# Three embedding products of the expert stage, put at other places in the instruction order

## The reference, cut to what matters

```python
h = h + hier_moe(rms_norm_2(h, g_ffn), w_rg, w_re, w1, w3, w2)
h = h + rms_norm_2(p @ w_ple, g_ple) * jax.nn.sigmoid(rms_norm_2(h, g_plg) @ w_plg)

def expert_block(args):          # for each block of tokens and its expert e
    xb, e = args
    hdn = jax.nn.silu(xb @ w1[e]) * (xb @ w3[e])
    return hdn @ w2[e]
```

## Time and profile before

| what | value |
|---|---|
| median of 3 runs | 1590.42 us (1586.77 to 1594.16) |
| the profiled execution | 1589.49 us, its span 1587.5 us |
| busy share of the span: PE, DVE, ACT, POOL | 96%, 45%, 33%, 10% |
| mean traffic, whole span | 196 GB/s |
| traffic from 1128 us to 1463 us | 420 to 421 GB/s |
| 1 MB weight loads from SP, issue to landing | 10.2 us median |

### The profile page before, as it was taken

How to read it: one execution, slowest core, us unless ns; L and a number is a source line. 1 busy time by engine, 2 the same in 40 slices (tenths; PEclk the granted TensorE clock), 3 DMA queues, 4 the chain that set the end, 5 groups by cost and what they waited for, 6 DMA issues and landing times.

```text
span 1587.5 us, 19637 instructions
## 1 busy us (share of the span) xinstructions
PE 1524.3 (96%) x7802; PEld 1065.2 (67%) x7802; DVE 717.9 (45%) x1208; ACT 530.8 (33%) x910; POOL 163.4 (10%) x172
## 2 busy tenths in 40 slices
PE   5899999999999999999999988999999999999898
PEld 5666688889888888888777766745444444444367
DVE  5344423455444444468665787532132132132174
ACT  4334422354332423345355676431011011010042
POOL 1013110002111111111300210011000000000000
PEclk9999999999999999999999999999999999999999
DMA  7111332213222222222110222779999999999951
GB/s 273 37 70 60 144 108 104 95 60 114 107 106 82 104 84 102 106 93 84 52 52 27 102 112 80 304 289 390 421 422 421 421 421 420 420 420 420 422 237 54
DMA packets 45437, 311.22 MB, mean 196 GB/s; under 512 B 5136, under 2 KB 5648, under 8 KB 10016
## 3 DMA queue, kind: packets, MB, share of 16 engines
q1 hardware_dynamic: 42336, 296.22, 46.8%
q0 software_dynamic: 3008, 13.72, 2.4%
HBM read 301.52 MB, written 8.39 MB: 195 GB/s over the span
## 4 chain that ended last, share of the span: by engine, by line
PE 88%; DVE 4%; ACT 3%; DMA 3%; issue 2%; DVEq 0%; ACTq 0%; POOLq 0%
PE bank L788 21%; PE bank L2463 14%; PE bank L832 8%; PE bank L1389 7%; PE bank L2479 6%; PE bank L841 5%; PE bank L2446 4%; PE bank L2496 4%; PE bank L2662 3%; PE bank L1246 3%; DMA M<-in_w 2%; PE bank L801 2%; PE bank L858 1%; PE bank L1782 1%; PE bank L717 1%
## 5 line engine op out<-in xcount | busy, mean ns | idle before, releaser
L612 DVE TENSOR_TENSOR w_lo<-M,w_hi 128x2048 fp32r<-128x2048 f32 x73 | 168.7, 2317 | 177.8 <-ACT w_hi L607 177.8
L2463 PE MATMUL bank<-M 128*64 128x512 f32 x1024 | 227.4, 595 | 4.3 <-DMA M<-in_w 4.3
L607 ACT ACTIVATE w_hi<-M 128x2048 fp32r<-128x2048 f32 x73 | 139.0, 1912 | 148.4 <-PE bank L788 56.9
L788 PE MATMUL bank<-HTH,w_hi 128*128 128x512 f32 x432 | 168.1, 389 | 0.0
L788 PE MATMUL bank<-HTL,w_hi 128*128 128x512 f32 x432 | 168.1, 389 | 0.0
L788 PE MATMUL bank<-HTH,w_lo 128*128 128x512 f32 x432 | 168.0, 389 | 0.0
L2463 PEld LDWEIGHTS bank<-M 128*64 128x64 f32 x1024 | 71.3, 137 | 140.0 <-issue 138.8
L2479 PE MATMUL bank<-M 128*64 128x512 f32 x512 | 114.0, 595 | 1.8 <-DMA M<-in_w 1.8
L2621 DVE TENSOR_TENSOR X<-bank,X 128x512 f32<-128x512 f32 x69 | 46.6, 689 | 113.8 <-PE bank L2496 113.7
L788 PEld LDWEIGHTS bank<-HTH,w_hi 128*128 128x128 f32 x432 | 81.1, 188 | 16.9
L788 PEld LDWEIGHTS bank<-HTL,w_hi 128*128 128x128 f32 x432 | 81.1, 188 | 16.8
(11 more groups left out here) (365 smaller groups left out, 2846.2 us busy)
## 6 DMA issues: line engine op xcount, KB each, us to landing
M<-in_w SPq DMA_DIRECT2D x192, 1024.0 KB, 10.2
M<-in_wd SPq DMA_DIRECT2D x78, 1024.0 KB, 4.8
M<-in_nb SPq DMA_DIRECT2D x4, 1536.0 KB, 6.6
X<-in_x SPq DMA_DIRECT2D x4, 512.0 KB, 9.9
M<-in_rows POOLq DMA_DIRECT2D x4, 512.0 KB, 6.2
M<-in_tb POOLq DMA_DIRECT2D x8, 256.0 KB, 4.0
rowb<-in_rows POOLq DMA_DIRECT2D x4, 512.0 KB, 5.2
xs_parts<-XSH POOLq DMA_DIRECT2D x1, 2048.0 KB, 10.1
```

Source lines behind the costliest of these rows:

```text
L607: e.activation(hi[:, :], slots[slot_of[n]], ACT.Copy).then_inc(split_hi_done, 1)
L612: e.tensor_tensor(lo[:, :], slots[slot_of[n]], hi[:, :], ALU.subtract).then_inc(split_lo_done, 1)
L788: m = e.matmul(out[:, :], w[:, k0 + k, n0:n0 + 128], v[k], start=(k == 0 and i == 0), stop=(k == len(hi) - 1 and i == 2))
L2463: m = e.matmul(b[64 * s:64 * s + 64, :], Xe[:, 4 * kh + k, o + C * s:o + C * s + C], unit_w(key, 4)[:, k, :], start=(kh == 0 and k == 0), ...
```

## The change

The three products that stood between the first gather and the steps of pairs 0 and 1 stand elsewhere: ("pl", 2, 1) behind the second quarter of group 1's gather and ahead of ("down", 0), ("pl", 3, 0) behind ("up", 1, 2) and its gather, and ("pl", 3, 1) behind ("up", 3, 2). ("pl", 2, 1) takes its PSUM bank from the common rotation instead of the routing's list. Nothing is computed differently, and each byte is moved as often as before.

```diff
-        MOE = [("one_hot", 0)] + [("gx", 0, kp) for kp in range(4)] + [("pl", 2, 1)]
+        MOE = [("one_hot", 0)] + [("gx", 0, kp) for kp in range(4)]
...
             if i == 0:
-                MOE += steps_of(0, 0) + [("pl", 3, 0)] + steps_of(0, 1) + [("pl", 3, 1), ("gs", 0), ("gs", 1), ("one_hot", 1), ("tu", 0)]
-                MOE += steps_of(1, 0) + gather(0) + steps_of(1, 1) + gather(1) + steps_of(1, 2) + gather(2, 3) + turned
+                MOE += steps_of(0, 0) + steps_of(0, 1) + [("gs", 0), ("gs", 1), ("one_hot", 1), ("tu", 0)]
+                MOE += steps_of(1, 0) + gather(0) + steps_of(1, 1) + gather(1) + [("pl", 2, 1)] + steps_of(1, 2) + gather(2, 3) + turned
...
-            MOE += steps_of(p, 0) + gather(0) + scatter(i - 2, 5) + steps_of(p, 1) + scatter(i - 2, 6, 7)
+            late = [[("pl", 3, n)] if i == 1 else [] for n in range(2)]
+            MOE += steps_of(p, 0) + gather(0) + late[0] + scatter(i - 2, 5) + steps_of(p, 1) + late[1] + scatter(i - 2, 6, 7)
...
-            if what == "gx" and at[0] == 0 or (what, *at) == ("pl", 2, 1):
+            if what == "gx" and at[0] == 0:
```

## The result

The changed kernel takes 1594.85 us in the median of 20 runs (1590.44 to 1597.71), the kernel before 1589.32 us in 20 runs (1583.73 to 1594.25). The ratio is 1.0031, with a 95% interval of [1.0022, 1.004]: within the half per cent that was called "same", in the range, and 1.9 us above the forecast of 1593 us. By the ratio the change costs 4.9 us, where 2.7 was forecast. That the median comes as near to 1593 is in part luck: the three runs that the forecast built on have a median 1.1 us above that of all 20. The profiled execution took 1591.9 us, forecast 1592.2; it is the fourth fastest of its 20, so that agreement is luck too.

A forecast was written before the change was run, and what follows sets the result against it. The weight stream was taken to set the end: load 36 0.7 us earlier, plus 3.4 us for POOL's transfers, gives +2.7 us, so 1592.2 us profiled and a median of 1593 us, 0.17% slower; range 1587 to 1598 us.

The forecast's parts named there:

- same: Outcome class: within about 0.5% (8 us) of the kernel before, what a measurement can tell from no change; chance 0.90.
- What bounds the kernel: Expert stage: the weight stream, full from 1128 us, sets the end; 1 us later there moves the end 1 us.
- PE's path: Start of expert stage: first step 1.0 us earlier after a 0.7 us wait, ("up", 1, 1) 4.8, ("up", 3, 2) 1.0 earlier.
- Load 31: Weight load waiting for the first half of ("up", 3, 2): issued at 1110.0 us, landing 4.8 us later.
- POOL's transfers: Store of tile 3 and gain load, issued near 1118 us in the full stream, cost it 3.4 us.
- The rival of hidden transfers: POOL's transfers fit between weight packets near 1118 us, load 36 lands 0.7 us earlier, median 1589.7 us; chance 0.2.
- the head start counts whole: Rival: the 4.8 us gained at ("up", 1, 1) go on into the weight stream, 1585.6 us; chance 0.08.
- The rival that the store of tile 2 holds DVE: DVE's selection for group 2 waits for a slow store, costing 1.7 us more, 1595 us; chance 0.12.
- the first step stays where it was: Rival: a wait for ACT's copy keeps the first step at 1048.5 us; median 1594 us; chance 0.1.
- 0.7 us earlier than before: Load 36, without POOL's transfers, lands at 1127.3 us instead of 1128.02 us.
- The store of tile 2 was to fit into a hole: Issued near 1086 us, before loads 23 and 24, at no cost; without the hole 1.7 us.
- nothing was counted for the clock: PE's 0.7 us pause before the first step, and longer pauses at stage end, leave granted clock at 1.00: 0 us.

The follow-up runs named there:

- e6: Changed kernel with the embedding weight in a place used once and POOL's store of tile 3 and gain load cut to 16 bytes per row: ratio 1.0003.
- e12: Changed kernel with POOL's stores of tiles 2 and 3 and the gain load all cut to 16 bytes per row: ratio 1.0007.
- e3: Changed kernel with POOL's store of tile 3 and gain load cut to 16 bytes per row: ratio 1.002.
- e8: Kernel before with only POOL's store of tile 3 and gain load issued late, behind one-hot matrix 2: ratio 1.0017.
- e11: Changed kernel with only the store of tile 2 cut to 16 bytes per row: ratio 1.002.
- e10: The changed kernel itself, run again: ratio 1.0029 to the kernel before.
- e2: Changed kernel with ("pl", 2, 1) back ahead of the first step, only tile 3's two products moved: ratio 1.0019.
- e4: Changed kernel with the embedding weight loaded into a place that takes one load only: ratio 1.0003.
- e7: Changed kernel with the embedding weight in a place used once and the gain load moved behind ("up", 3, 15): ratio 1.0014.

## Why the prediction was right, and which term was off

**What bounds the kernel.** Shown. PE had its head start of 4.4 us at ("up", 1, 1), and the end came later all the same, with the stream. In every kernel but e6 the time at equal clock follows the delay-free chain of load 36 within 1.1 us. A single trace follows less closely: from the landing of load 36 to the end the 14 traces take 458.6 to 461.9 us.

**PE's path.** Right. The first step starts 0.7 us earlier against G (1.0 forecast), after a pause of 0.99 us (0.7 forecast), ("up", 1, 1) 4.4 (4.8), ("up", 3, 2) 1.0 us earlier (1.0). The stretch from 1045.5 to 1050 us shows the granted clock at 1.00 through the pause.

**Load 31.** Right: issued at G + 63.6, forecast G + 63.5; it took 5.2 us (forecast 4.8), and 4.8 in e12.

**POOL's transfers.** Right: 3.2 us at loads 34 to 36, forecast 3.4; e3 and e8 show that they are the cause. The rival of hidden transfers is refuted by these two, and that the head start counts whole by the end at G + 544.3 us. The rival that the store of tile 2 holds DVE didn't occur, nor the one that the first step stays where it was.

**The term that was off** is the "0.7 us earlier than before" at load 36. Load 36 of after was reckoned without delays (1127.3 us, G + 80.8) and set against load 36 of before as its trace had it (1128.02 us, G + 81.5). That trace holds 1.4 us of irregular delays, at loads 24, 25 and 35. Reckoned alike, before is at 80.1, and the term is +0.7 instead of -0.7. The sum then is +0.7 + 3.2 = +3.9 us instead of +2.7, against +4.0 ± 0.6 and +3.9 ± 0.8 measured at equal clock; of the 4.9 us of the ratio it leaves 1.0 us, which may be the clock's. So the late place costs a little more than the head start pays; the forecast had it a little less.

**Two smaller readings were off.** The store of tile 2 was to fit into a hole ahead of loads 23 and 24; it went out 0.8 us ahead of load 23 and delayed it by 2.8 us (e11). And nothing was counted for the clock, which fell behind the wait for load 36; in the profiled execution that cost no time, since the end moved by 3.3 us and load 36 by 3.2.

**Open** are how much of the store of tile 2 reaches the end (0 to 1.1 us), what sets off the irregular delays, why e6 stays behind its chain, and whether the clock's fall costs the change time in other executions.

## What to carry to other kernels

Where a stream of loads sets the end, put a price on each move by the load that it delays: its issue, the time of a load alone, and the loads behind it at the stream's rate; work that leaves the busy engine's path is worth only what that load gains. Reckon before and after in the same way, since a trace holds delays that a sum leaves out. A transfer of another engine costs its share of the stream wherever the stream is full, so issue it in a hole; and a buffer that is held longer is held from every load behind it.

## What the runs showed of the hardware that was not expected

Single loads in the full stream come 0.3 to 2.4 us late, beyond what POOL's transfers explain: in before loads 24 and 25 landed 0.4 and 1.5 us more than 2.49 us behind the one ahead. Some places recur: load 27 or 28, near G + 60 us, came 1.0 to 2.4 us late in eight of the 14 traces and in time in the other six. Many delays, not all, lie beside a packet of instructions on another queue; that these cause the delays was not tested. Here are the queues from 1089 to 1102 us of before, the stretch of those two loads (packets, MB, share of 16 engines):

```profile
q1 hardware_dynamic: 717, 5.23, 100.7%
q8 instruction: 1, 0.02, 0.4%
```

The granted clock fell behind the long wait of PE for load 36 in after, though the forecast counted nothing for the clock. The windows, columns as in the earlier trace rows:

```profile
1127.80:1130.50 2.70, 0.00 (x0) 0.00 (x0) 0.00 (x0) 0.00 (x0) 0.00 (x0) 1.00 0.99 410
1130.50:1133.20 2.70, 2.64 (x10) 1.17 (x12) 0.00 (x0) 0.00 (x0) 0.00 (x0) 0.73 1.01 428
1133.20:1135.90 2.70, 2.70 (x9) 0.65 (x5) 0.00 (x0) 0.00 (x0) 0.00 (x0) 0.64 1.03 434
1135.90:1140.00 4.10, 4.10 (x27) 3.62 (x28) 1.39 (x2) 0.70 (x2) 0.00 (x0) 1.00 1.00 418
```

At 0.73 and 0.64, means between the two levels of 2.4 and 1.2 GHz, the half step took 5.35 us instead of the 3.65 us of before. In e10, e2 and e11 the half step at this place took 5.35, 5.16 and 5.35 us behind waits of 2.7, 2.4 and 2.9 us. In e8 and e4 it took 3.65 us behind 2.6 and 2.2 us, and in e7 the clock fell behind 2.1 us. So the length of the wait alone didn't tell which would happen. In after the 1.7 us came out of the waits ahead of the end, 4.1 us instead of 5.6, and so cost nothing there; in e7, behind the last of these waits, they came on top.
